# A product of ones behind each tile of the input's transposes, in a one-core decoder layer

## The reference

```python
def mixer_inputs(x, norm_g, w_in, lb, qn_g, kn_g):
    bsz, length, _ = x.shape
    u = rms_norm(x, norm_g) @ w_in
...
        oa, st_p = hgrn2_scan(qa, lf, ka, va, jnp.zeros((bp, A_HEADS, A_DK, A_DV), jnp.float32))
        oa = hgrn2_output(oa, hgrn_norm[l], ga, xp.dtype)
        ob = swa_prompt(qb, kb, vb, attn_sinks[l], bias_p, mask_p)
        xp = xp + jnp.concatenate([oa, ob.astype(xp.dtype)], axis=-1) @ w_out[l]
        xp = swiglu(xp, norm_ffn[l], w_gate[l], w_up[l], w_down[l])
...
def swiglu(x, g, wg, wu, wd):
    h = rms_norm(x, g)
    return x + (jax.nn.silu(h @ wg) * (h @ wu)) @ wd
```

## Time and profile before

| | us |
|---|---|
| median of 3 runs | 1367.4 |
| lowest and highest | 1365.98, 1367.83 |
| the profiled execution, whole | 1367.65 |
| its span, first to last instruction | 1365.9 |
| TensorE busy | 1352.0 |
| VectorE busy | 768.2 |
| ScalarE busy | 533.0 |
| mean granted clock of TensorE | 0.991 |

### The profile page before, as it was taken

How to read it: one execution, slowest core, us unless ns; L and a number is a source line. 1 busy time by engine, 2 the same in 40 slices (tenths; PEclk the granted TensorE clock), 3 DMA queues, 4 the chain that set the end, 5 groups by cost and what they waited for, 6 DMA issues and landing times.

```text
span 1365.9 us, 25119 instructions
## 1 busy us (share of the span) xinstructions
PE 1352.0 (99%) x11030; PEld 1317.2 (96%) x11030; DVE 768.2 (56%) x976; ACT 533.0 (39%) x615; POOL 117.0 (9%) x153
## 2 busy tenths in 40 slices
PE   9999999999999999999999999999999999999998
PEld 7999999898899999999999999999999999999998
DVE  5346765588737566446464555546464555545464
ACT  6337975323244344333333333333333333333331
POOL 2010430213200350000000000000000000000000
PEclk8999999899999999999999999999999999999999
DMA  9795545546853555555565565555565565555552
GB/s 286 198 311 156 162 130 151 154 112 180 245 201 124 185 155 155 163 177 155 161 179 155 173 166 156 164 175 155 163 177 155 168 171 156 164 174 155 164 176 71
DMA packets 320744, 231.42 MB, mean 169 GB/s; under 512 B 5126, under 2 KB 292111, under 8 KB 320314
## 3 DMA queue, kind: packets, MB, share of 16 engines
q1 hardware_dynamic: 314432, 206.19, 52.6%
q0 software_dynamic: 6112, 23.59, 5.3%
q10 hardware_dynamic: 90, 0.02, 0.0%
HBM read 219.99 MB, written 14.97 MB: 172 GB/s over the span
## 4 chain that ended last, share of the span: by engine, by line
PE 95%; DMA 2%; DVE 2%; issue 1%; ACT 1%; SPq 0%; ACTq 0%; DVEq 0%
PE acc L1514 29%; PE acc L1518 29%; PE acc L1515 28%; DMA raw<-in_w_in_dram 1%; PE mx L1464 1%; PE mx L1690 1%; PE acc L1528 1%; DMA reg_qkf<-in_x_sample_dram 1%; PE mx L1613 0%; PE mx L1585 0%; PE mx L1659 0%; DVE wl L973 0%; PE mx L1993 0%; PE mx L1773 0%; PE mx L1600 0%
## 5 line engine op out<-in xcount | busy, mean ns | idle before, releaser
L1514 PE MATMUL acc<-act_h,wh 128*128 128x288 f32 x2208 | 596.9, 299 | 1.1 <-ACT wh L628 1.1
L1515 PE MATMUL acc<-act_l,wh 128*128 128x288 f32 x2208 | 593.7, 295 | 0.0
L628 ACT ACTIVATE wh<-raw 128x2048 fp32r<-128x2048 f32 x192 | 366.8, 1911 | 248.3 <-PE acc L1518 234.5
L973 DVE TENSOR_TENSOR wl<-raw,wh 128x2048 fp32r<-128x2048 f32 x192 | 440.2, 2293 | 11.5 <-ACT wh L628 8.1
L1514 PEld LDWEIGHTS acc<-act_h,wh 128*128 128x128 f32 x2208 | 415.5, 188 | 7.2 <-issue 5.0
L1515 PEld LDWEIGHTS acc<-act_l,wh 128*128 128x128 f32 x2208 | 415.0, 188 | 0.0
L1518 PE MATMUL acc<-act_h,wl 128*128 128x288 f32 x2208 | 322.1, 298 | 0.0
L1518 PEld LDWEIGHTS acc<-act_h,wl 128*128 128x128 f32 x2208 | 302.1, 189 | 4.7 <-issue 3.3
L1514 PE MATMUL acc<-mix_h,wh 128*128 128x288 f32 x832 | 228.3, 299 | 0.0
L1515 PE MATMUL acc<-mix_l,wh 128*128 128x288 f32 x832 | 227.7, 295 | 0.0
L1514 PEld LDWEIGHTS acc<-mix_h,wh 128*128 128x128 f32 x832 | 157.1, 189 | 1.7 <-issue 1.7
(11 more groups left out here) (265 smaller groups left out, 714.6 us busy)
## 6 DMA issues: line engine op xcount, KB each, us to landing
raw<-in_w_in_dram SPq DMA_DIRECT2D x44, 1024.0 KB, 5.9
raw<-in_w_gate_dram SPq DMA_DIRECT2D x44, 1024.0 KB, 5.6
raw<-in_w_up_dram SPq DMA_DIRECT2D x44, 1024.0 KB, 5.7
raw<-in_w_down_dram SPq DMA_DIRECT2D x44, 1024.0 KB, 5.1
raw<-in_w_out_dram SPq DMA_DIRECT2D x16, 1024.0 KB, 5.4
reg_x<-in_state_hgrn_dram POOLq DMA_DIRECT2D x16, 256.0 KB, 6.3
out_dram<-reg_x POOLq DMA_DIRECT2D x16, 256.0 KB, 3.5
bias_rows<-bias_line POOLq DMA_DIRECT2D x1, 3072.0 KB, 16.9
```

The source lines that it names most:

```text
L628: nc.scalar.activation(wh[:, s % WH, :], raw[:, s % RAW, :], ACT.Copy).then_inc(high_done, 1)
L973: nc.vector.tensor_tensor(wl[:, s % WL, :], raw[:, s % RAW, :], wh[:, s % WH, :].bitcast(F32), ALU.subtract).then_inc(low_done, 1)
L1514: mm(out, w_h[:, i, cols], a_hi[:, place(i), :], start=(i == 0), stop=False)
L1515: mm(out, w_h[:, i, cols], a_lo[:, place(i), :], start=False, stop=False)
```

## The change

`warm` gets the bank as an argument; the products of ones write to `acc[0]`, the bank of unit 0, instead of `mx`'s first. Behind each `x_transpose(k)` one such product is added, sixteen in all.

```diff
             pe.wait_ge(ones_set, 1)
-            def warm(n):
+            def warm(n, bank):
                 for _ in range(n):
-                    mm(mx[:, 0, 0:P], ones, ones, start=True, stop=True)
-
-            warm(10)
+                    mm(bank[:, 0:P], ones, ones, start=True, stop=True)
+
+            warm(10, acc[0])
             pe.wait_ge(small_in, 16)
             pe.wait_ge(gain_in, 16)
             nc.tensor.transpose(acc[3][:, 0:KD], param_rows[0:KD], ident[0:KD, 0:KD]).then_inc(gain_t, 1)
-            warm(10)
+            warm(10, acc[0])
             for k in range(KD):
                 x_transpose(k)
+                warm(1, acc[0])
```

## The result

The changed kernel takes 1378.44 us (median of 5 runs, 1375.15 to 1380.22), the kernel before 1367.22 us (5 runs, 1362.3 to 1367.83): ratio 1.0098, interval [1.0077, 1.0119]. That is +11.2 us where +6.8 was forecast, and 0.1 us above the range. Measured twice more, the ratio was 1.0097 [1.007, 1.0124] and 1.0064 [1.004, 1.0088].

The account below looks back on a forecast made before the run. TensorE bounds the kernel, its start at half clock. Added products delay unit 0 by 6.7 us, its passes add 0.1: +6.8 on 1367.65 gives 1374.45, forecast as 1374.2 us for the median; range 1365.5 to 1378.3.

Parts of the forecast that it names:

- The forecast of 28 us for unit 0: Kernel start: unit 0's first pass begins at 28.2 us, +6.7 us, after the last tile's transpose and product.
- a constant shift behind it: After unit 0's start: everything comes later by a constant 6 to 7 us.
- the sum's way from sixteen products to +6.8 us: Start: 3.4 tiles at 0.77 us, 11.6 at 1.29, last product 0.43, first passes +0.1; total +6.8 us.
- all of it through: After 22 us: no wait has a date of its own, so all +6.8 us reaches the end.
- 0.43 us: Behind each transposed tile: price of one added product at half clock; 0.23 us at full clock.
- tile 0's last transpose stays at 9.68: Start of the tiles: the change leaves tile 0's last transpose at 9.68 us.
- the fall at 12.3 us: Among the transposes: the clock falls at 12.3 us as before, at full product price; chance 0.72.
- The passes at half clock, "+0.1": Unit 0's dense passes: 0.8 us more at half speed costs 0.4 us; +0.1 us taken.
- why the clock falls: Transposes at the start: they don't count as busy like products; the clock stayed 0.50 through 9.20 us of busy transposes.
- The row on idle gaps: Skill text cited for the stays-up rival: throughput drops come from idle gaps; with products no gap exceeds 0.54 us.
- The rival "the clock stays up": Transposes at 9.7 to 21 us: added products keep the clock at 1.00, -1.8 us, 1365.6 us; chance 0.19.

Follow-up runs that it names:

- The two fillings: Kernel before, wait for x_sample filled with sixteen products of ones instead of ten (1361.03 us, ratio 0.9968), or with twelve added transposes (1361.81 us, ratio 0.997).
- the three fillings: Kernel before with sixteen products ahead (1361.03 us) or twelve added transposes (1361.81 us); the change with sixteen products ahead instead of ten (1365.48 us).
- the runs with 1.31 us at a held clock: Kernel before with thirteen products of ones ahead of the transposes instead of ten: 1363.82 us, ratio 0.9986 [0.9965, 1.0007].
- the bank alone: The change without its sixteen added products, products of ones still writing to acc[0], against the kernel before: 1367.74 us, ratio 1.0001 [0.9985, 1.0016].
- the filling with sixteen products: Kernel before with sixteen products of ones instead of ten ahead of the transposes: 1361.03 us, ratio 0.9968 [0.9953, 0.9982].

## Why the prediction was right and wrong

**Right: the direction and the mechanism in the queue.** The clock was at 0.50 from 12.4 us on, one product a tile did not lift it, and all of TensorE's extra time reached the end (9.8 us at 31 us, 9.84 us at 240 us). The forecast of 28 us for unit 0 and of a constant shift behind it has this form.

**The step that failed** is the sum's way from sixteen products to +6.8 us. The product's price was taken too low, and the term "all of it through" left nothing for what the longer queue does near 290 us. Of the 5.2 us by which the profiled execution missed the sum, about 3.1 arose in the first 31 us and 2.2 behind 240.

**Mis-sized: the price of a product, "0.43 us".** I took the pace of products behind products. Among transposes a product costs 0.53 us at half clock (1.40 - 0.86) and 0.27 at full. Over the 12 to 13 tiles at half clock this is 1.3 us. The last product costs 0.73 us and not 0.43 before unit 0 (31.27 - 30.03 against 21.51 - 21.00). Together 1.6 us.

**Wrong by chance of the execution: "tile 0's last transpose stays at 9.68".** It was at 10.49; the repeats of the change have 9.61 and 9.50. This is 0.8 us of that profile, and one tile more at half clock, 0.6 us. It is luck, and so is how well the fall at 12.3 us was met: in the two repeats the clock fell at 11.0 and 11.3 us, which puts one or two tiles more at half clock, and unit 0 started 9.2 and 8.9 us later than before.

**The passes at half clock, "+0.1"**: the low pass of unit 1 is 10.03 us later where unit 0 started 9.76 us later, so 0.3.

**Wrong: "I find no wait with a date of its own after 22 us, so I let all of it through".** What came through was more: the stop of about 2 us at L1702 came in all profiled executions of the change, and it was gone in the one with six more products. The third fall of the clock behind it cost 1.6 us, of which the shorter second one gave back 0.9. I had looked for waits that could swallow time and not for what 32 more matmuls, and as many weight loads, do to TensorE's queue. On balance it is 2.2 us in the profile of after (0.8 and 1.5 in the two repeats).
So 6.8 + 1.6 + 1.4 + 0.2 + 2.2 = 12.2 us, against 12.0 measured between the two profiles.

**Wrong: why the clock falls.** The prediction read the rows as if transposes let the clock fall and only products hold it. The two fillings show otherwise: transposes alone hold 1.00 for 8.6 us if TensorE was not idle just before. At 0.50 they don't bring it back; nor does one product a tile. The wait for x_sample, which stands in both kernels, is what let it fall: with the wait filled the clock held through the tiles in 29 of the thirty executions of the three fillings, judged by their times and mean clocks (of one, 1365.64 us at 0.994, they don't tell). But the products among the transposes are not without effect, as two a tile held the clock in eight executions of ten; one a tile was too little to change the odds (2 of 20 executions, and 4 of 8 with six more behind the last tile, against 22 of 99 of the kernel before). The Trainium skill, "TensorE: Matmul & The Clock Gate", section "Part 4: PE-mode transpose", says that transposes don't engage the full clock; this trace agrees for raising it and not for holding it. The row on idle gaps in "Why this matters for your kernels", which I had put as a rival's support, was nearer to the cause: I had applied it to the gaps between the products, and it is the gap ahead of the tiles that counts (1.24 us in the kernel before), though the runs with 1.31 us at a held clock and with two products a tile show that it does not decide alone.

**The rival "the clock stays up" was mispriced, and it is real**: 2 of 20 executions of the change, at 1366.16 and 1367.03 us against the 1365.6 that I gave it (each product costs 0.27 us among transposes and not 0.23, 0.6 us in all). But the kernel before has it too. Of its executions in the later rounds, taken together, 22 of 99 are under 1364 us. One product a tile thus made a held clock no more frequent. So at a held clock the change is slower as well, by about 5 us, the price of sixteen products.

## What to carry to other kernels

Before paying for work that is meant to keep TensorE's clock up, find what stood right before the fall: here it was an idle wait of 1.2 us, and filling it, even with transposes nobody reads, gains 0.3%. One product a tile in the busy stretch behind it costs 0.3% at full clock and makes 1% at half; two a tile mostly held the clock, but cost slightly more than that saved. Price an added instruction by its pace among the instructions that it will stand between, not by its pace among its own kind. And a kernel whose executions fall in two groups needs ten or more of them before one profile of it is trusted.

## What the runs showed that I had not expected

- Transposes keep the granted clock at 1.00 for 8.6 us (9.49 to 18.11) when the engine is busy before them, though 8.9 us of them at 0.50 don't raise it (12.3 to 21.2).
- In the profile with two float32 products behind each three transposes the clock came back after about 10 us at 0.50, and in eight of ten executions it seems never to have fallen; one product did not bring it back in 18.7 us.
- TensorE's "issue" stop near 270 to 290 us stands at a fixed place of its instruction queue (before the 4477th or the 4986th to 4987th matmul or weight load) and so before another product when instructions are added ahead of it: 1.18 us in the kernel before, 0.9 with the bank alone, 1.9 to 2.3 in the change, none in the filling with sixteen products. Each ends 1.39 to 1.54 us after a 16 KB load of instructions lands. That the stop is a wait for this load is read from the traces and was not tried by an experiment.
